# A hybrid attention layer on one core: the probabilities are multiplied by their coefficients on GpSimd instead of VectorE

## The reference

```python
u = rms_norm(h, pre_norm[l])
proj = jnp.einsum('bsd,de->bse', u, w_in[l])
qa, ka, va, ga, qb, kb, vb, gb, qc, gc = jnp.split(proj, IN_SPLITS, axis=-1)
# A: 6 heads, causal window of 128, a learned sink in the denominator
oa, _ = banded_attention(qa * scale, ka, va, A_WINDOW - 1, sink)
# B: 6 heads, three (window, dilation) pairs, weighted by their denominators
for (win, dil) in ((128, 1), (512, 4), (2048, 16)):
    o, lse = banded_attention(qs, to_strided(kb, dil), to_strided(vb, dil), win // dil, None)
wts = jax.nn.softmax(jnp.stack(lses, axis=0), axis=0)
ob = jnp.sum(wts[..., None] * jnp.stack(outs, axis=0), axis=0)
# C: 4 heads, all tokens against 256 memory tokens
pc = jax.nn.softmax(jnp.einsum('bshd,bmhd->bhsm', qc * scale, mk), axis=-1)
oc = jnp.einsum('bhsm,bmhd->bshd', pc, mv)
y = jnp.concatenate([oa * jax.nn.silu(ga), ob * jax.nn.silu(gb), oc * jax.nn.silu(gc)], axis=-1)
y = jnp.einsum('bse,ed->bsd', y, w_out[l])
h = h + rms_norm(y, post_norm[l])
```

## Time and profile before

| | |
|---|---|
| median of 3 runs | 2163.92 us (2161.46 to 2164.92) |
| profiled execution, first to last instruction | 2163.3 us |
| mean granted TensorE clock | 0.973 |
| PE busy | 2054.7 us, 95% |
| PE weight loads busy | 1717.7 us, 79% |
| DVE busy | 1557.3 us, 72% |
| ACT busy | 1351.1 us, 62% |
| POOL busy | 114.9 us, 5% |

### The profile page before, as it was taken

How to read it: one execution, slowest core, us unless ns; L and a number is a source line. 1 busy time by engine, 2 the same in 40 slices (tenths; PEclk the granted TensorE clock), 3 DMA queues, 4 the chain that set the end, 5 groups by cost and what they waited for, 6 DMA issues and landing times. The chain is left out here.

```text
span 2163.3 us, 39340 instructions
## 1 busy us (share of the span) xinstructions
PE 2054.7 (95%) x12892; PEld 1717.7 (79%) x12892; DVE 1557.3 (72%) x4410; ACT 1351.1 (62%) x3520; POOL 114.9 (5%) x116
## 2 busy tenths in 40 slices
PE   5999899999999999999899999999899998999998
PEld 4787678888888888888777887888778887788886
DVE  6564674546664574446588989989799997888887
ACT  6454454544555464343699979989689998533333
POOL 1232310000000000002000000000000000000000
PEclk7999999999999999999799989989999999999999
DMA  4477576777577657589778676686869996245543
GB/s 157 144 243 217 170 240 179 221 242 218 154 225 223 219 182 244 199 276 273 179 147 157 133 142 135 131 166 121 166 149 214 232 270 179 98 158 175 174 158 113
DMA packets 351737, 401.40 MB, mean 186 GB/s; under 512 B 105617, under 2 KB 255249, under 8 KB 346689
## 3 DMA queue, kind: packets, MB, share of 16 engines
q1 hardware_dynamic: 343120, 364.80, 61.5%
q0 software_dynamic: 8432, 34.30, 5.1%
HBM read 255.62 MB, written 143.39 MB: 184 GB/s over the span
## 5 line engine op out<-in xcount | busy, mean ns | idle before, releaser
L854 PE MATMUL p_ps<-p_u_hi,p_w_hi 128*128 128x512 f32 x1344 | 534.7, 398 | 25.8 <-DVE p_p_c L739 10.6
L856 PE MATMUL p_ps<-p_u_hi,p_w_lo 128*128 128x512 f32 x1344 | 526.8, 392 | 0.0
L855 PE MATMUL p_ps<-p_u_lo,p_w_hi 128*128 128x512 f32 x1344 | 526.2, 392 | 0.0
L570 DVE TENSOR_TENSOR p_w_lo<-p_w_raw,p_w_hi 128x512 fp32r<-128x512 f32 x336 | 245.7, 732 | 331.4 <-ACT p_w_hi L423 329.8
L1621 ACT ACTIVATE probs<-probs,a_stat 128x256 f32<-128x256 f32 (+1 forms) x896 | 433.7, 489 | 49.2 <-DVE a_stat L1455 45.8
L423 ACT ACTIVATE p_w_hi<-p_w_raw 128x512 fp32r<-128x512 f32 x336 | 210.7, 628 | 331.7 <-PE p_ps L856 303.7
L854 PEld LDWEIGHTS p_ps<-p_u_hi,p_w_hi 128*128 128x128 f32 x1344 | 254.1, 189 | 86.1 <-DVE p_u_lo L577 12.0
L856 PEld LDWEIGHTS p_ps<-p_u_hi,p_w_lo 128*128 128x128 f32 x1344 | 254.0, 189 | 54.5
L1455 DVE CUSTOM_DVE_ANT_0 probs<-a_ps_s,fixed 128x256 f32<-128x256 f32 (+1 forms) x704 | 251.6, 396 | 63.2 <-PE a_ps_s L1354 61.9
L855 PEld LDWEIGHTS p_ps<-p_u_lo,p_w_hi 128*128 128x128 f32 x1344 | 254.4, 189 | 50.7
L1408 PE MATMUL a_ps_o<-a_pT,a_v 128*64 128x128 f32 x3320 | 256.7, 285 | 22.8 <-ACT a_pT L1645 21.5
(11 more groups left out here) (202 smaller groups left out, 2756.5 us busy)
## 6 DMA issues: line engine op xcount, KB each, us to landing
p_w_raw<-in_w_in SPq DMA_DIRECT2D x156, 256.0 KB, 3.6
p_w_raw<-scratch_w_s SPq DMA_DIRECT2D x144, 256.0 KB, 3.7
scratch_qk_hi<-p_out_a SPq DMA_DIRECT2D x80, 256.0 KB, 4.1
scratch_qk_lo<-p_out_b SPq DMA_DIRECT2D x80, 256.0 KB, 4.2
a_v<-scratch_v SPq DMA_DIRECT2D x40, 512.0 KB, 7.6
scratch_gate<-p_out_a SPq DMA_DIRECT2D x64, 256.0 KB, 3.9
scratch_v<-p_out_a SPq DMA_DIRECT2D x256, 64.0 KB, 2.3
a_gate<-scratch_gate SPq DMA_DIRECT2D x64, 256.0 KB, 5.9
```

The lines of the kernel that those rows point to most:

```text
L570: nc.vector.tensor_tensor(w_lo[:, m % 3, :, :], w_raw[:, entry(j, g), :, :], w_hi[:, m % 3, :, :].bitcast(F32), ALU.subtract).then_inc(w_l ...
L854: nc.tensor.matmul(bank, hi, u_hi[j][:, k, :], start=j < 2 and k == 0, stop=False, skip_group_check=True)
L855: nc.tensor.matmul(bank, hi, u_lo[j][:, k, :], start=False, stop=False, skip_group_check=True)
L856: last = nc.tensor.matmul(bank, lo, u_hi[j][:, k, :], start=False, stop=k == KH - 1, skip_group_check=True)
```

## The change

`scale` is taken out of DVE's queue and given to GpSimd's, as a `tensor_scalar` of the same shape in a new function `pool_parts`. A new `pool_round` goes through the same slots, and calls `scale` alone. Its only wait is on `coef_ready` before a phase's first slot; the counter `weighted`, for which PE waits, is now raised by GpSimd. GpSimd's seven DMAs are issued between phases (`then_load`), with their old waits but for the four of L1921, whose counts are lower by one phase. The rest of DVE's, ACT's and PE's queues stays as it was.

```diff
-        def scale(phase, e):                       # in vector_parts
-            if e == 0:
-                dve.wait_ge(coef_ready, p + 1 + C1)
-            for j in range(2):
-                last = nc.vector.tensor_scalar(place, place, coef[:, s, u.column:u.column + 1], None, ALU.mult)
-            last.then_inc(weighted, 1)
...
+    def pool_parts(pool):
+        def scale(phase, e):
+            p, s = number(phase), phase[1]
+            if e == 0:
+                pool.wait_ge(coef_ready, p + 1 + (kind == "A"))
+            for j in range(2):
+                u = FLAT[s][2 * e + j]
+                place = probs[:, s, 2 * e + j, 2 * P - u.keys:]
+                last = nc.gpsimd.tensor_scalar(place, place, coef[:, s, u.column:u.column + 1], None, ALU.mult)
+            last.then_inc(weighted, 1)
...
-                if slot.ahead:                     # in vector_round
-                    x, e = slot.ahead
-                    x.parts.scale(x.phase, e)
...
+        def pool_round(a, c, b):
+            for slot in slots_of(a, c, b):
+                if slot.ahead:
+                    x, e = slot.ahead
+                    x.parts.scale(x.phase, e)
+                    if e == x.g.NP - 1:
+                        x.parts.then_load(x.phase)
...
-                for n in range(4):
-                    pool.wait_ge(A.done_sem, (9 + n) * NC)
-                    load_sum(n)
-                for n in range(3):
-                    pool.wait_ge(C.done_sem, (1 + n) * NC)
-                    load_w(n)
+                def then_load(g):
+                    def load(phase):
+                        n = 2 * phase[0] + phase[1]
+                        if g is A and n >= 8:
+                            pool.wait_ge(A.done_sem, n * NC)
+                            load_sum(n - 8)
+                        if g is C and 2 <= n < 5:
+                            pool.wait_ge(C.done_sem, (n - 1) * NC)
+                            load_w(n - 2)
+                    return load
+                rounds(pool, pool_round, lambda g: named(scale=g.pool_parts(pool).scale, then_load=then_load(g)))
```

More of the change, by code:

```diff
@@ L1432, in vector_parts @@
             dve.wait_ge(coef_ready, 1)
-        C1 = 1 if kind == "A" else 0
         def scores(phase, slot):
@@ L1534, in exchange @@
                                      mybir.AxisListType.X).then_inc(coef_ready, 1)
-        def scale(phase, e):
-            h, s = phase
-            p = number(phase)
-            if e == 0:
-                dve.wait_ge(coef_ready, p + 1 + C1)
-            for j in range(2):
-                u = FLAT[s][2 * e + j]
-                place = probs[:, s, 2 * e + j, 2 * P - u.keys:]
-                last = nc.vector.tensor_scalar(place, place, coef[:, s, u.column:u.column + 1], None, ALU.mult)
-            last.then_inc(weighted, 1)
         def copy_queries(phase, slot):
@@ L1609, in gated @@
             nc.vector.tensor_tensor(by, summed.rearrange("p u (r a) -> p u r a", a=32), by, ALU.mult).then_inc(y_ready, 1)
-        return named(scores=scores, exchange=exchange if kind == "B" else inverse, scale=scale, finish=finish, finish_rest=finish_rest, gated=gated, copy_queries=copy_queries)
+        return named(scores=scores, exchange=exchange if kind == "B" else inverse, finish=finish, finish_rest=finish_rest, gated=gated, copy_queries=copy_queries)
     def scalar_parts(act):
@@ L1675, in scalar_parts @@
         return named(scores=scores, exchange=exchange, copy=copy, keep=keep, copy_queries=copy_queries)
+    def pool_parts(pool):
[8 more added lines that the diff above has]
+            last.then_inc(weighted, 1)
+        return named(scale=scale)
     return named(
@@ L1681, in head_group @@
         q_copied=q_copied, copied_by=copied_by, natural_copied=natural_copied,
-        loads=loads, tensor_parts=tensor_parts, vector_parts=vector_parts, scalar_parts=scalar_parts)
+        loads=loads, tensor_parts=tensor_parts, vector_parts=vector_parts, scalar_parts=scalar_parts, pool_parts=pool_parts)
 def load_y(sp, sc, ahead, i, b, rows=(0, KD // 2)):
```

## The result

The changed kernel takes 2215.97 us (median of 4 runs, 2210.53 to 2219.01), beside it the kernel before 2162.69 us. The ratio is 1.0233, 95% interval 1.0208 to 1.0258: about 50 us slower, where 40 us faster had been forecast. The profiled execution spans 2216.6 us, 53.3 us more than before. One execution of the kernel before, at 4,130 us beside e5 to e7, was a slow one and is left out of every ratio.

A forecast was written before the change was run, and what follows sets the result against it. ACT was taken as the floor of the attention stage, kept waiting by DVE's maxima; -34 us (maxima) - 6 (clock) + 0 (GpSimd) = -40, so 2163.9 - 40 = 2124 us, range 2098 to 2161.

The forecast's parts named there:

- the price of a multiplication on GpSimd: GpSimd in the attention stage: 0.40 us for 256 elements, 0.80 a slot, hidden, so adding 0 us.
- the upper bound of 0.87: Highest GpSimd price for 256 elements, from a two-tensor addition of 512 taking 1.75 us beside a loaded DVE.
- GpSimd as the bound: Rival at `weighted`, for which every turn waits: GpSimd becomes the bound, 2251 us at 1.0 us a unit; chance 13%.
- its formula: That rival's unit-price limits by group: 0.73 us in C, 0.85 in A, 0.94 in B; net turns at about 0.92.
- the relief of 34 + 6 us: Attention stage: 34 us from ACT's waits for DVE's maxima, 6 us from one stretch less at half clock.
- the 28 us of relief: Cross-check in group B: 4.7 of a possible 6.5 us per pair of phases, over six heads, gives 28 us.
- What bounds the kernel: Attention stage: ACT is the floor, its idle 74.8 us the ceiling of gain, 45.8 of them waits for DVE's maxima.
- The clock: Thin PE slots in B halve the granted clock; one stretch less, 6 us, between 0 and 14.
- DVE beside GpSimd: Attention stage: the maxima stay at 0.42 us, two-SBUF-input instructions take at most 1.1 us each; cost nothing.
- The rival of 7%: DVE's maxima and GpSimd's multiplications exclude each other at the port, 1.64 us a slot: no gain, 2160 us; chance 7%.
- GpSimd's DMAs: Three loads of L1927 behind a phase's multiplications, up to 12 us later, 1805, still before ACT's need at 1830.17: covered.

The follow-up runs named there:

- e5: e3 with GpSimd waiting before each slot until PE has turned the slot four before; 2128.85 us, ratio 0.9832 to the kernel before.
- e7: Changed kernel, but GpSimd multiplies in group B alone and DVE multiplies in A and C; 2179.28 us, ratio 1.0064 to the kernel before.
- e2: Changed kernel with a constant in place of the coefficient in GpSimd's tensor_scalar; 2150.83 us, ratio 0.9926 to the kernel before.
- e3: Changed kernel with GpSimd's tensor_scalar replaced by tensor_tensor, the coefficient repeated as second input; 2331.96 us, ratio 1.0767 to the kernel before.
- e1: Changed kernel with GpSimd multiplying only the last 16 columns of each unit; 2128.13 us, ratio 0.9817 to the kernel before.
- e6: Changed kernel with each slot shared: GpSimd multiplies the first unit, DVE the second; 2157.54 us, ratio 0.9962 to the kernel before.
- e9: e3 with one more, already met wait before each slot on GpSimd; 2324.63 us, ratio 1.0759 to the kernel before.

## Why the prediction was wrong

**The failed step is the price of a multiplication on GpSimd.** I took 0.40 us for 256 columns, "nearest to the copy"; it is 0.90, more than the upper bound of 0.87, and 0.58 for 128 (bound 0.44). The reasoning counted inputs: one tensor must cost what a copy costs, and two at most what the contended addition costs. The runs say that inputs are not the measure. tensor_scalar costs 2.5 ns a column with or without a coefficient to read (e2), and tensor_tensor with a repeated second input 1.66 (e3). The rows bounded other instructions, and were taken as bounds of this one. Nor was 1.75 us the longest addition of 512 columns in the trace of before: L949 has one of 3.33 us at 55.90.

**GpSimd as the bound** was the rival on the slower side, with 13%, with the right place (`weighted`, every turn). But its formula was too mild as well: at the measured 0.90 us it gives 27 us of loss against 40 of relief, so still a gain of 13, about 2,151 us. It turned only at 0.94 (0.92 with the 34 us alone), and its +87 us at 1.0 left the relief out. A second step failed there. I set the relief of 34 + 6 us and GpSimd's price side by side and added them, but a phase takes the longer of the two. In B the multiplications alone are 75 x 0.90 + 21 x 0.58 = 79.7 us for two phases, against 80.75 before: no loss, as the formula said, but almost none of the 28 us of relief either. By the same formula 0.90 us cost A (1.80 - 1.71) x 96 = 9 and C (1.80 - 1.51) x 64 = 19 us; measured are 20.7 and 18.7, and 8 more at the end. It had left out four things: the time for which DVE's instructions hold up GpSimd's, 3 us in each pair of B's phases, which made 82.8 of 79.7; the round in which A follows B, where 43 us of B's last multiplications (48 x 0.90) stand before A's first (34.7 to 44.5 us in that round); the tail, which has no scores to hide in and goes at 1.80 us a slot where it went at 1.02; and GpSimd's own DMAs, 0.8 us each in the queue that is now the longest, which make three of C's phases 15.2 us instead of 14.4.

**What bounds the kernel, and what the relief is worth: right.** e1 measured 39.7 us (33 to 46) for the 40 forecast; B's two phases 77.0 us for 76, ACT's waits for maxima 13.6 us for "under 12" (7.3 of them a load), A about 0.1 us a slot, as forecast, and C unchanged at 12.19. In e5 ACT is at 96.5% in B for the 97% foreseen.

**The clock: right in sign.** The kernel before has two stretches at half clock inside B, of 17 and 14 us. The changed kernel has one of 17, one stretch less as counted, and e5 only 3 us near 1,488, so that from 1100 to 1500 its clock is 1.00 for 0.96. e6, where DVE stays full around 1,255, has three. What the stretches alone are worth was not isolated.

**DVE beside GpSimd: right for the maxima, wrong for the multiplications.** The maxima, with one input in PSUM, last as long as before:

```profile
L1453 DVE CUSTOM_DVE_ANT_0 probs<-a_ps_s,fixed 128x256 f32<-128x256 f32 x569 | 217.5, 421 | 167.8 <-PE a_ps_s L1354 156.7 <-PE a_ps_t L1424 2.5 <-DVE a_ps_s L1495 1.0
```

421 ns for 420. L1596, with two inputs in SBUF, took at most 1.13 us in the changed kernel. So DVE's side cost nothing that shows, as forecast. But the prediction asked only what GpSimd does to DVE. The hold-up went the other way too, onto the engine that had become the bound: 21 us of GpSimd's time. That these 21 us come from DVE's instructions is read from their meeting in the trace; no run isolates it. That L1596 would be held for 18 us by a faster instruction on GpSimd was not foreseen either. The rival of 7% had the maxima take turns with the multiplications, which no run shows; what does take turns are L1596 and the casts, and e3 is the extreme case of it: ACT's 179 us of waits.

The Trainium skill, Perfetto Trace Analysis, § Optimizing Scalar/DVE Operations, warns that moving work between GpSimd and VectorE might not help, since they share a read port. e3 agrees with it (18.3 us in flight for 0.69 of work), and so do the changed kernel's 21 us; the maxima do not bear it out. The Trainium skill, GPSIMD Engine Reference, § Performance versus the Vector engine, was nearer to the price than my 0.40 us: by its factor of about two the estimate was 0.70 us, and the measured ratio is 940 / 348 = 2.7. Had I taken that value for the sum, the sum would have kept its sign.

**GpSimd's DMAs** were not late for ACT, as forecast, but they held up the multiplications behind them.

## What to carry to other kernels

Before work is moved to an engine that has never done it in this kernel, measure one such instruction at two widths; a row of another operation bounds nothing here, and from the point where the new engine is the longest queue its time is paid nearly in full (65 of 75 us in e2). Relief and price are not added: each phase takes the longer of the two queues. Moving work off an engine can pay even when that engine is not the floor (39.7 us in e1, with DVE busy 213 us less), through the waits it causes and perhaps through the clock, whose share was not isolated. Look at what two engines do to each other in both directions. Where GpSimd runs tensor_tensor beside VectorE instructions with two inputs in SBUF, as in e3 and e5, it needs pauses, and a wait that is already met is not a pause (e9).

## What the runs showed of the hardware

- GpSimd, 128 partitions, float32, start to start: tensor_scalar 0.26 us + 2.5 ns a column with a coefficient from SBUF (0.296 us for 16 columns, 0.58 for 128, 0.90 for 256), 0.174 us + 2.5 ns with a constant; tensor_tensor with a step-0 second input 0.145 us + 1.66 ns.
- A VectorE instruction with two SBUF inputs was in flight until GpSimd's unbroken run of tensor_tensor ended: up to 18.3 us for 0.69 us of work, and always until 0.55 us after the run's end (11 cases in e3, 11 in e9). Beside tensor_scalar on GpSimd it took at most 1.13 us, and there GpSimd's multiplication was the one that grew: 0.92 to 1.23 us for 256 columns, 0.60 to 1.14 for 128. Why one run of instructions lets it in and the other doesn't is open; that only the fixed part of tensor_scalar leaves the port free would fit, and was not tested.
- VectorE's own tensor_scalar became slower beside GpSimd's: 348 ns alone, 398 in e6.
